# One 2 MB weight transfer near the end of a mixture-of-experts layer is split by rows into five transfers

## What is computed

```python
def expert_mlp(x, w1, b1, w2, b2):
    u = x @ w1 + b1                              # w1: 1024 x 2048 per expert
    x_glu = jnp.minimum(u[..., ::2], SWIGLU_LIMIT)
    x_lin = jnp.clip(u[..., 1::2], -SWIGLU_LIMIT, SWIGLU_LIMIT)
    return (x_glu * jax.nn.sigmoid(SWIGLU_ALPHA * x_glu) * (x_lin + 1.0)) @ w2 + b2   # w2: 1024 x 1024
```

## Time and profile before

| | |
|---|---|
| median of 3 runs (lowest, highest) | 1182.65 us (1182.26, 1182.7) |
| the profiled execution's own time | 1185.93 us |
| span of the profiled execution, first to last instruction | 1183.7 us |
| TensorE matmul busy | 1147.2 us, 97% of the span |
| SP's load queue | 434.19 MB, 88.2% of 16 DMA engines' span |
| read from device memory | 436.38 MB, 372 GB/s over the span |

### The profile page before, as it was taken

One profiled execution on the slowest core, in us unless ns is written; L12 is line 12 of the kernel. 1 busy time (PEld: TensorE's weight loads), 2 busy tenths in 40 slices (PEclk: granted clock), 3 DMA queues, 4 the chain that ended last, 5 costly groups with the idle time before them and its releaser, 6 DMA issues.

```text
span 1183.7 us, 14356 instructions
## 1 busy us (share of the span) xinstructions
PE 1147.2 (97%) x6226; PEld 570.2 (48%) x6226; DVE 375.1 (32%) x774; ACT 179.2 (15%) x330; POOL 28.8 (2%) x54
## 2 busy tenths in 40 slices
PE   8999999999999999999999998999898999999997
PEld 7689997544434343434344343434342434343433
DVE  4568776423312122222232221212121212121222
ACT  2344133012101110101011010101010101010111
POOL 3220000000000000000000000000000000000000
PEclk9999999999999999999999999999999999999999
DMA  9533348948999999999999999999999999999995
GB/s 299 151 93 111 117 169 280 424 203 345 422 434 429 431 432 428 434 434 427 428 435 430 431 430 431 429 434 428 434 431 429 429 436 428 429 433 424 427 426 206
DMA packets 45969, 440.03 MB, mean 372 GB/s; under 512 B 3790, under 2 KB 21552, under 8 KB 29760
## 3 DMA queue, kind: packets, MB, share of 16 engines
q1 hardware_dynamic: 43760, 434.19, 88.2%
q0 software_dynamic: 1904, 4.10, 1.2%
q10 hardware_dynamic: 240, 0.79, 0.2%
HBM read 436.38 MB, written 3.67 MB: 372 GB/s over the span
## 4 chain that ended last, share of the span: by engine, by line
PE 69%; DMA 28%; issue 1%; ACT 1%; DVE 1%; ACTq 0%; DVEq 0%
DMA ring<-in_w 27%; PE ps L1255 23%; PE ps L1318 14%; PE ps L793 8%; PE ps L1340 4%; PE ps L1021 3%; PE ps L1120 3%; PE ps L1043 2%; PE ps L753 1%; PE ps L730 1%; PE ps L1270 1%; PE ps L1128 1%; ACT xnT L1699 1%; PE ps L1282 1%; PE ps L1047 1%
## 5 line engine op out<-in xcount | busy, mean ns | idle before, releaser
L1255 PE MATMUL ps<-ring,hnT 128*64 128x512 f32 x2032 | 451.9, 601 | 14.2 <-DMA ring<-in_w 14.2
L1255 PEld LDWEIGHTS ps<-ring,hnT 128*64 128x64 f32 x2032 | 144.1, 138 | 305.7 <-issue 282.6
L1318 PE MATMUL ps<-ring,xnT 128*64 128x512 f32 x992 | 218.9, 593 | 7.0 <-DMA ring<-in_w 7.0
L2238 DVE TENSOR_TENSOR xnT<-ps,b1T 128x512 f32<-128x512 f32 x32 | 22.1, 692 | 421.9 <-PE ps L1270 421.9
L1318 PEld LDWEIGHTS ps<-ring,xnT 128*64 128x64 f32 x992 | 73.7, 137 | 147.8 <-issue 146.9
L1686 ACT COPY hnT<-ps 128x1024 f32<-128x1024 f32 x32 | 32.4, 1012 | 507.6 <-PE ps L1255 507.6
L2259 DVE TENSOR_TENSOR acc<-acc,ps 128x1024 f32<-128x1024 f32 x30 | 36.6, 1218 | 227.0 <-PE ps L1340 210.8
L1340 PE MATMUL ps<-xnT,cst 128*128 128x512 f32 (+1 forms) x180 | 76.0, 619 | 1.4
L1120 PE MATMUL ps<-cst,region 128*128 128x128 f32 x512 | 61.9, 278 | 0.7 <-issue 0.7
L1120 PEld LDWEIGHTS ps<-cst,region 128*128 128x128 f32 x512 | 58.5, 192 | 2.8 <-issue 0.9
L1698 ACT COPY xnT<-ps 64x512 f32<-64x512 f32 x31 | 17.9, 578 | 244.2 <-PE ps L1318 244.2
(11 more groups left out here) (312 smaller groups left out, 830.3 us busy)
## 6 DMA issues: line engine op xcount, KB each, us to landing
ring<-in_w SPq DMA_DIRECT2D x74, 4096.0 KB, 36.0
ring<-in_w SPq DMA_DIRECT2D x31, 2048.0 KB, 34.7
ring<-in_w SPq DMA_DIRECT2D x20, 1024.0 KB, 11.0
ring<-in_w_in SPq DMA_DIRECT2D x17, 1024.0 KB, 5.2
ring<-in_w_o SPq DMA_DIRECT2D x2, 2048.0 KB, 10.9
ring<-in_w SPq DMA_DIRECT2D x8, 512.0 KB, 23.0
ring<-in_w_b SPq DMA_DIRECT2D x1, 2048.0 KB, 11.5
ring<-in_w_a SPq DMA_DIRECT2D x4, 512.0 KB, 6.2
```

The costliest lines, as they stand in the source:

```text
L1255: mm = pe.matmul(ps[o:o + 64, bank + q // 2, into].rearrange("p (j x) -> p j x", x=4), stationary, columns[:, q], start=(at == 0), stop=(a ...
L1318: mm = pe.matmul(ps[64 * c:64 * c + 64, 6, :], hT[:, which, order_of(f), :], ring[:, slot, D * (f % 2) + 512 * c:D * (f % 2) + 512 * c + 512],
L2238: dve.tensor_tensor(glu, ps[:, 2, :].rearrange("p (f t) -> p f t", f=KF), wide(b1T[:, bass.ds(e, 1), 0, :].rearrange("p a f -> p (a f)").u ...
```

## The change

The load of the second half of chunk 92 (the chunk "four from the end"; steps 2 and 3 of w1 of expert 31) is issued as five transfers over the same bytes: one of rows 0 to 95 and four of eight rows each. All five raise the same semaphore by 16, and TensorE waits for 64 more on it. Nothing else differs.

```diff
+DEALT = (len(CHUNKS) - 4, 2)
+ROW_PARTS = ((0, 96), (96, 104), (104, 112), (112, 120), (120, 128))
...
                 if kind == "w1":
-                    sp.dma_start(room(i, half), w1v[e, h, half]).then_inc(chunk_in[i % ROOMS][2 * half], 16)
+                    for r0, r1 in ROW_PARTS if (i, 2 * half) == DEALT else ((0, P),):
+                        sp.dma_start(room(i, half)[r0:r1], w1v[e, h, half][r0:r1]).then_inc(chunk_in[i % ROOMS][2 * half], 16)
...
                         elif (i, k % 4) in LANDED:
-                            pe.wait_ge(chunk_in[i % ROOMS][k % 4], 16 * LANDED[i, k % 4])
+                            more = 16 * (len(ROW_PARTS) - 1) if (i, k % 4) == DEALT else 0
+                            pe.wait_ge(chunk_in[i % ROOMS][k % 4], 16 * LANDED[i, k % 4] + more)
```

## The result

The changed kernel took 1196.16 us (median of 4 runs, 1195.01 to 1197.87), the kernel before 1182.56 us (4 runs, 1182.26 to 1182.7). The ratio is 1.0116, 95% interval 1.0104 to 1.0128: 13.6 us slower. The profiled execution took 1196.21 us, close to its median; the one of before was 3.28 us above its own.

A forecast was written before the change was run, and what follows sets the result against it. PE and weight loading run nearly level, the end set by a landing at 1156 us. Relieving the late engines gives -1.22 us, other terms 0: from 1182.65 to 1181.4 us, range 1181.0 to 1184.2 us.

The forecast's parts named there:

- What bounds the kernel: Whole run: PE and loading nearly level, the end set by a transfer's landing at 1156 us.
- path from landing to end: Last expert: later landings move with the split transfer's engines, PE's starts follow, and the end moves by 1.22 us.
- one row of 16,384 bytes takes 0.61 us: Split transfer: one engine moves 26.9 GB/s, so each row moved between engines costs or saves 0.61 us.
- ±1.22 us on one half of the engines: Split transfer: eight engines carry 10 rows, 1.22 us more; eight carry 6, 1.22 us less.
- a fixed cost per transfer: Four added transfers: at most 0.11 us each, 0.45 us together; taken as 0 and kept for the range.
- Eight rows on eight engines: Split transfer: each eight-row transfer runs on eight engines with a row each, the same eight each time.
- the rival of few engines: Eight-row transfers run on four engines, 1186.3 us, or on one, 1193 to 1201 us; chance 0.06.
- Late half relieved or burdened: Engines finishing last get 6 rows, -1.22 us, chance 0.47; or they, or one of the last two, get ten, chance 0.32.
- the burdened case: Rival: the late half, or one of the two last engines, gets ten rows; +1.22 us, 1183.9 us; chance 0.32.
- SP's issues, the wait, the fixed cost: Four more issues, some 1.7 us, hidden by SP's waiting; PE's wait for 64 more free; fixed cost taken as 0.
- What would show it wrong: Time moving by more than 2.4 us either way, or landings behind the split transfer not moving at all.
- the sign of few engines: Split transfer lands more than 3 us later and PE waits for it after its first 16 matmuls.

The follow-up runs named there:

- transfer (4): Kernel before plus single awaited transfers after the outputs are stored; this one writes 96 rows of 16 KB into partitions 0 to 95: 9.00 us.
- columns: Changed kernel with its five transfers cut by columns, all 128 rows in each: 1182.96 us, ratio 1.0005 to the kernel before.
- two_parts: Changed kernel with two transfers by rows, 96 and 32, instead of five: 1193.95 us, ratio 1.010 to the kernel before.
- transfer (5): Kernel before plus single awaited transfers after the outputs are stored; this one writes eight source rows into partitions 96 to 103: 3.72 us.

## Why the prediction was wrong

*What bounds the kernel: right.* The end is set by landings, every later transfer moves with the one before it, and the waits at lines 1260 and 1323 moved together by 10.43 and 10.45 us. The prediction's path from landing to end held.

*The step that failed: "one row of 16,384 bytes takes 0.61 us", taken for every transfer.* The prediction took a rate measured on transfers of 128 rows and moved rows between engines at that price, so that a sum over counts of rows was all there was to do. The runs showed in its place that the price belongs to the set of rows that a transfer writes: a row takes 0.61 us in transfers of 128 rows and in that of rows 32 to 95, but 1.27 us in that of rows 0 to 63, with 96 rows alone about 1.1 us (an estimated 231 GB/s, transfer (4)), and in the stream a median of 1.21 us, which is 180 to 295 GB/s for 25 us. Where the prediction had ±1.22 us on one half of the engines, all sixteen lost some 12 us. No rival had this mechanism. The prediction's remark that a fixed cost per transfer might be 0.11 us looked for the price in the number of transfers, and columns and two_parts show that it isn't there.

The Trainium skill has a sentence that speaks against the change and that the prediction passed over (DMA: Bandwidth & Descriptors, section "The descriptor swizzle"): in a transfer to 128 partitions each of the 16 engines writes one port of its own. By the map of ports that the Trainium skill gives (SBUF — State Buffer, the section named above) a transfer of rows 0 to 95 can't use all 16 ports evenly. The runs agree in what can be seen from outside: the one cut by columns is free, every cut by rows costs, and which rows stand together decides how much. That engines in the changed transfer wait at a port which the neighbour's rows need at the same moment, and so hold up the neighbour's rows queued behind theirs, is argued from 5.5 slow MB against 2.1 changed MB, and from PE's wait for the transfer ahead of the split one; no row names an engine or a port.

*Eight rows on eight engines: right for a transfer alone.* By the packet records the eight rows of transfer (5) start within 0.07 us of each other and take 0.97 to 1.10 us each. At full rate the packets' times add up to a share of 1.00, which is one packet at a time on each of the 16 engines; by that measure eight packets at once are eight engines with a row each. One engine with all eight rows would need 4.9 us. That it is the same eight each time, no record shows. So the rival of few engines isn't the reason; that its time (1193 to 1201 us) holds the measured one is luck.

*Late half relieved or burdened: not decided.* The change is 1.6 us further above before than two_parts (13.6 and 12.0 us, from different series). That is the size and the sign of the burdened case, 1.22 us, but other sources of 1 us can't be excluded, and the sign of so small a term was what the prediction spent most of its thought on.

*SP's issues, the wait, the fixed cost: right that they cost nothing.* Columns shows it for all together, with as many transfers, the same waits and semaphore counts. The size of the issues was wrong: the prediction had 1.7 us for four more, and in the changed kernel the four eights held SP for 2.01, 1.74, 1.18 and 1.18 us, together 6.1 us. The load behind them was still issued at 1100.96 us.

*What would show it wrong.* The prediction named a move of more than 2.4 us, and it was 13.6 us. It also named the split transfer's own late landing as the sign of few engines. The landing did come late: PE's wait for it ended at 1152.13 us, and the transfer of before landed at 1141.4 us. But the sign was not the cause. The DMA share beside GB/s tells the two apart: with few engines each row would still take 0.61 us, and GB/s would fall only where the share falls; here GB/s fell to half at a share of 1.0.

## What to carry to other kernels

In a stream like this one, which keeps the DMA engines full, try a split by columns before one by rows: five transfers of 128 rows were free, and two of 96 and 32 rows cost 12 us on 2 MB, with more than half of the slow bytes in the transfers next to them. A DMA microsecond lost in this stream reached the end whole, at each of the three places tried. Look at the DMA share and GB/s together: here a full share at half the rate was engines in each other's way, not engines with too much to do.

## What was not expected of the hardware

A transfer of 1 MB to rows 32 to 95 took 5.38 us and the same bytes to rows 0 to 63 took 7.56 us, each row 1.27 us instead of 0.61. While one split transfer of 2 MB landed, 5.5 MB went at half the rate, its own bytes among them. And the loss isn't the sum of bytes through ports: taken together, the parts of every cut by rows write the same rows with the same bytes as the whole transfer, and still lost between 6 and 12 us.
